# When the last LayerNorm sum is read, and where six h_lo subtractions stand in VectorE's queue

## The chip, the cores and the metric

One core of one Trainium2 chip. The metric is device time in microseconds, the median of several executions. TensorE (PE) multiplies, VectorE (DVE) and ScalarE (ACT) work elementwise, GpSimd (POOL) here does one kind of subtraction, and the sync engine (SP) issues most loads. The kernel is written engine by engine: each engine has a fixed list of instructions, and semaphores are the only thing that holds one engine for another.

## The reference

One mixer layer over x of 512 x 2048 floats, everything in fp32:

```python
h = rmsnorm(x, pre_norm_g)
q, fz, iv, gate_a, u, ug, gate_b = split(h @ w_in)            # 7 blocks of 1024 columns
# group A: 8 heads of a gated linear recurrence (HGRN2), d_k = d_v = 128
o_a = hgrn2(q, fz, iv, lower_bound) -> per-head rmsnorm * norm_g * silu(gate_a)
# group B: GLU, causal depthwise convolution of width 31, LayerNorm over the 1024 channels
a = u * sigmoid(ug);  y = conv31(a) + bias
o_b = silu((y - mean(y)) * rsqrt(var(y) + eps) * g + b) * silu(gate_b)
out = x + rmsnorm(concat(o_a, o_b) @ w_out, post_norm_g)
```

## The kernel before

**Precision.** Every large product runs as three fp32r products, hi x hi, hi x lo and lo x hi. Each operand is thus cut in two: ACT copies the raw tile to the `hi` tile (L374 for weights, L602 for the mixer's output) and a subtraction gives the `lo` tile (POOL L324 for weights, DVE L1011 in `mix_lo` for the mixer's output).

**Units.** Weights come as 144 units of 512 KB through a ring of four slots: 48 units for the convolution's channels (they also bring the value columns), 64 for the heads (8 a head), 32 for the output product (4 column blocks `c`, 8 units `s` each). A unit is 24 matmuls of 512 columns, issued 0.227 us apart. Per unit: SP loads it, ACT makes w_hi (`hi_unit`, two units ahead), POOL makes w_lo, PE multiplies.

**Stages.** (1) x is normalised and transposed; (2) convolution channels; (3) `head(0)` to `head(7)`: PE projects head h while the small matmuls of head h-1 (`slot(h-1, u)`) come after unit u, and DVE and ACT do that head's `late(h-1, u)` and their `own(h, u)`; (4) the output product, where the small matmuls of head 7 (`slot(7, s)`) come ahead of unit s of block c = 0.

**The LayerNorm statistics.** In head 0, at u = 5, DVE centres the 8 tiles (L781). At u = 6 and 7 ACT squares them one after the other (L459) into t1 and t2, and DVE adds them into t3 (L791, L789). The 8 adds count up `vacc_done`; t1 and t2 are used in turn, so each square waits for the add of the one before last. PE sums t3 over the partitions with an fp32 matmul against ones into bank 3 (L1253, `var_done`), and ACT turns that into 1/std in `lnr` (`ln_rstd`, L463 and L465). `lnr` is used first by DVE at u = 4 of head 1.

**Block c = 0 of the output product.** `mix` holds 16 tiles of the mixer's output. Tile `at` (in the order MIX_AT) becomes h_hi by ACT's `mix_hi(at)` (semaphore `mhi_done`) and h_lo by DVE's `mix_lo(at)` (`mlo_done`). Unit s of PE waits for `mlo_done >= 2 s + 2`. Meanwhile head 7 must be finished on the same engines. PE's `slot(7, s)` for s = 1, 2, 3 waits for `probs_done` counts 4, 6 and 12 of that head, which DVE reaches by copying masked scores out of PSUM (`take_scores`: L920 and L915 give 1 to 4, L928 gives 5 and 6, L935 gives 7 to 12, L941 the last). The last LayerNorm tile (`ln_tile(7, ...)`, DVE L799 to L814, ACT L472 to L480) runs between them. ACT's queue there is, in order: six L602; the gate (L539 to L382); L374, two L602 (tiles 6, 7); L374, L546, L548, two L602 (8, 9); L374, L551; L472, L473, L475, L477; two L602 (10, 11); L374; L480; one L602 (12).

Of the kernel before, what the change touches and what calls it, by code (L numbers as in the profile page):

```python
# [27 lines left out]
def build_layer(nc, x, pre_norm_g, post_norm_g, w_in, lb_logits, hg_norm_g, dw_kernel, dw_bias,  # L28
# [23 lines left out]
    CONV_U, HEAD_U = 2 * CONV_T, 2 * HEAD_T  # L52
# [36 lines left out]
    with ctx:  # L89
# [273 lines left out]
        def _(act):  # L363
# [97 lines left out]
            def ln_rstd():  # L461
                act.wait_ge(var_done, 1)
                A(lnr, bank(3), ACT.Ln, scale=1.0 / W_B, bias=EPSB).then_inc(lnr_s, 1)  # L463
                act.wait_ge(lnr_s, 1)
                A(lnr, lnr, ACT.Exp, scale=-0.5).then_inc(lnr_s, 1)  # L465

            def ln_tile(j, s):

                if s == 0:
                    act.wait_ge(gb_taken, j + 1)  # L470
                    act.wait_ge(ln_v, 7 * j + 2)
                    A(t3, t1, ACT.Abs).then_inc(ln_s, 1)  # L472
                    A(t4, gates[:, ds(j * T, T)], ACT.Abs).then_inc(ln_s, 1)  # L473
                    act.wait_ge(ln_s, 4 * j + 2)
                    A(part(2, 2), part(2, 2), ACT.Exp, scale=-1.0).then_inc(ln_s, 1)  # L475
                    act.wait_ge(ln_s, 4 * j + 3)
                    A(part(2, 2), part(2, 2), ACT.Ln, bias=1.0).then_inc(ln_s, 1)  # L477
                if s == 1:
                    act.wait_ge(ln_v, 7 * j + 5)
                    A(t3, t3, ACT.Exp).then_inc(ln_sig, 1)  # L480
# [53 lines left out]
            def late(g, u, first, last=False):  # L534
                if u == 0:
                    act.wait_ge(unit_done, N_HEAD + HEAD_U * (g + 1))
                    if not first:
                        act.wait_ge(head_done, g)
                    A(sgate, bank(1), ACT.Copy).then_inc(gate_taken, 1)  # L539
                    act.wait_ge(gate_taken, g + 1)  # L540
                    softplus_of_abs(sgate, t4, gate_s, 3 * g)
                if u == 1:
                    act.wait_ge(v_taken, H // 2)
                    if not first:
                        act.wait_ge(o_done, g)
                    A(vals, mix[:, ds(g * T, T)], ACT.Copy).then_inc(vals_ready, 1)  # L546
                    act.wait_ge(gate_ls, g + 1)
                    A(t4, t4, ACT.Exp).then_inc(gate_sig, 1)  # L548
                if u == 2:
                    act.wait_ge(kt_done, g + 1)  # L550
                    A(kdec[:, 0:T - P], XB[:, 0:T - P], ACT.Copy).then_inc(kt_taken, 1)  # L551
                if u == SQ_U:
                    act.wait_ge(o_done, g + 1)
                    act.wait_ge(gate_ready, g + 1)
                    act.wait_ge(ln_v, 7 * g + 6)
                    A(t4, OB, ACT.Square).then_inc(osq_done, 1)
                    if not last:
                        act.wait_ge(osq_done, 2 * g + 1)
                        A(sq_hi, t4, ACT.Copy).then_inc(osq_hi, 1)
                if u == 7:  # L560
                    act.wait_ge(norm_done, g + 1)
                    A(t1, XB, ACT.Ln, scale=1.0 / P, bias=EPSB).then_inc(rs_s, 1)
                    act.wait_ge(rs_s, 2 * g + 1)
                    A(t1, t1, ACT.Exp, scale=-0.5).then_inc(rs_s, 1)

            def head_step(h, u, q0, squares=None):
                base = N_HEAD + HEAD_U * h
                hi_unit(base + u + AHEAD, (u + AHEAD) % RING, q0 + (u + AHEAD) // RING,
                        squares=squares if u == SQ_U + 1 else None)
# [10 lines left out]
            def head_rest(h, first):  # L580
                for u in range(HEAD_U):
                    head_step(h, u, N_HEAD // RING + 2 * h, squares=h)
                    if first and u == 1:
                        ln_rstd()
                    late(h - 1, u, first)
                    own(h, u, False)
                    if u in (4, 5):
                        ln_tile(h - 1, u - 4)
# [66 lines left out]
        def _(dve):  # L655
# [137 lines left out]
            def ln_tile(j, s, first):  # L793
                y = mix[:, ds((H + j) * T, T)]
                gb = gates[:, ds(j * T, T)]
                if s == 0:
                    if first:
                        dve.wait_ge(lnr_s, 2)
                    V.tensor_copy(lnp[:, :], par3[:, TAPS + 1:TAPS + 3, j]).then_inc(ln_v, 1)  # L799
                    V.tensor_tensor(t1, y, lnr, ALU.mult).then_inc(ln_x, 1)  # L800
                    dve.wait_ge(ln_v, 7 * j + 1)
                    dve.wait_ge(ln_x, j + 1)
                    V.tensor_scalar(t1, t1, lnp[:, 0:1], lnp[:, 1:2], ALU.mult, ALU.add).then_inc(ln_v, 1)
                if s == 1:
                    dve.wait_ge(ln_s, 4 * (j + 1))
                    V.scalar_tensor_tensor(t3, t1, 0.0, t3, ALU.min, ALU.subtract).then_inc(ln_v, 1)
                    V.scalar_tensor_tensor(t4, gb, 0.0, t4, ALU.min, ALU.subtract).then_inc(ln_v, 1)
                    dve.wait_ge(ln_v, 7 * j + 4)
                    V.tensor_tensor(t3, t3, t4, ALU.add).then_inc(ln_v, 1)
                    V.tensor_tensor(t2, t1, gb, ALU.mult).then_inc(ln_v, 1)  # L810
                if s == 2:
                    dve.wait_ge(ln_sig, j + 1)
                    dve.wait_ge(ln_v, 7 * j + 6)
                    V.tensor_tensor(y, t2, t3, ALU.mult).then_inc(ln_v, 1)  # L814
# [192 lines left out]
            def mix_lo(at):  # L1007
                m = MIX_AT[at]
                dve.wait_ge(mhi_done, at + 1)
                a = slice(at * T, (at + 1) * T)  # L1010
                V.tensor_tensor(h_lo[:, a], mix[:, m * T:(m + 1) * T], h_hi[:, a].bitcast(fp32), ALU.subtract).then_inc(mlo_done, 1)  # L1011
# [9 lines left out]
                V.tensor_tensor(mix[:, tt * D + c * 512:tt * D + (c + 1) * 512], bank(4 * (c % 2) + tt),  # L1021
                                gates[:, c * 512:(c + 1) * 512], ALU.mult).then_inc(y_taken, 1)

            for at in range(4):
                mix_lo(at)
            for s in range(OUT_U):
                late(H - 1, s, False, last=True)
                if s == 1:
                    mix_lo(4)
                    mix_lo(5)  # L1030
                if s in (2, 3, 4):
                    ln_tile(J - 1, s - 2, False)
                for at in {2: (6, 7), 3: (8, 9), 4: (10, 11), 5: (12, 13), 6: (14,), 7: (15,)}.get(s, ()):
                    mix_lo(at)
            dve.wait_ge(gain_in, 32)
            for c in range(CHUNKS - 1):
# [16 lines left out]
        def _(pe):  # L1053
# [64 lines left out]
            def project(n, slot, half, b):  # L1118

                pe.wait_ge(lo_done, n + 1)  # L1120
                for k in range(HK):
                    kt = half * HK + k
                    wh = w_hi[:, slot * UW + k * P:slot * UW + (k + 1) * P]
                    wl = w_lo[:, slot * UW + k * P:slot * UW + (k + 1) * P]
                    hh, hl = h_hi[:, kt * T:(kt + 1) * T], h_lo[:, kt * T:(kt + 1) * T]
                    mm(bank(b), wh, hh, start=kt == 0, stop=False)  # L1126
                    mm(bank(b), wh, hl, start=False, stop=False)  # L1127
                    ins = mm(bank(b), wl, hh, start=False, stop=kt == KT - 1)  # L1128
                ins.then_inc(unit_done, 1)
# [105 lines left out]
            def head(h, first, second):  # L1235
                for u in range(HEAD_U):
                    if u == 0:
                        pe.wait_ge(ug_taken, J) if first else pe.wait_ge(gb_taken, h)
                    if u == 2:
                        pe.wait_ge(u_taken, J) if first else pe.wait_ge(gate_taken, h)  # L1240
                    if u == 4:
                        pe.wait_ge(f_v, 8 * h + 2)
                    if u == 6:
                        pe.wait_ge(q_taken, h + 1)
                    project(N_HEAD + HEAD_U * h + u, u % RING, u % 2, (u // 2) % 2)
                    if not first:
                        slot(h - 1, u, second)
                    if first and u == 4:
                        pe.wait_ge(ysum_done, J)
                        mm(bank(2), ones[:, :], lnr, start=True, stop=True).then_inc(mean_done, 1)  # L1250
                    if second and u == 0:
                        pe.wait_ge(vacc_done, J)
                        mm(bank(3), ones[:, :], t3, start=True, stop=True).then_inc(var_done, 1)  # L1253

# [65 lines left out]
```

## Time and profile before

| what | value |
|---|---|
| median of 3 runs | 890.32 us (890.29 to 892.9) |
| the profiled execution | 890.29 us, of it 888.3 us span from first to last instruction |
| PE busy | 872.4 us, 98% of the span |
| DVE busy | 567.7 us, 64% |
| ACT busy | 386.7 us, 44% |
| POOL busy | 363.5 us, 41%, of it 357.4 us in L324 |
| granted TensorE clock, mean | 0.992 |

The profile gives for each instruction its start, its length, and the idle time of its engine before it with what ended that. PEld is PE's weight load, which runs ahead of the matmul. Starts overlap the end of the instruction before by about 0.1 us on DVE and ACT. A matmul's length covers its way through the array; the step from one start to the next (0.227 us for 512 columns) is what it costs in a row.

### The profile page before, as it was taken

To read this page: it belongs to the slowest core of one execution; us is meant where nothing else is said; L and a number is where in the kernel's file an instruction comes from. 1 tells how busy PE (TensorE), PEld (TensorE's weight loads), DVE (VectorE), ACT (ScalarE), POOL (GpSimd) and SP (SyncE) were. 2 spreads that over 40 slices of the span, in tenths; PEclk is the share of its full clock that TensorE was granted. 3 is DMA by queue.
4 is the path that set the end of the run, shared out by engine and by line. 5 is a ranking of instruction groups with operands and counts; after the bars stand their busy time and mean duration, and the time that the engine had idled before them with its cause. 6 is when DMAs were issued, how large, how long until landed. Compare 5 with 4: busy or idle time off the path is not lost.

```text
span 888.3 us, 13244 instructions
## 1 busy us (share of the span) xinstructions
PE 872.4 (98%) x4616; PEld 747.8 (84%) x4616; DVE 567.7 (64%) x911; ACT 386.7 (44%) x585; POOL 363.5 (41%) x165
## 2 busy tenths in 40 slices
PE   6999999999999999999999999999999999999996
PEld 5998898898898888888888888888888888888885
DVE  6877786786786894775849486684948892010105
ACT  6433312312312455654746565573756743222221
POOL 3374444444444444352442435244242534444440
PEclk8999999999999999999999999999999999999999
DMA  9243233233233233132232314233132345433304
GB/s 317 69 128 102 80 104 103 78 104 102 77 105 101 78 95 96 48 116 74 72 94 70 96 47 121 68 88 91 57 94 63 101 140 209 153 100 101 101 5 190
DMA packets 119703, 89.70 MB, mean 101 GB/s; under 512 B 2640, under 2 KB 109433, under 8 KB 118137
## 3 DMA queue, kind: packets, MB, share of 16 engines
q1 hardware_dynamic: 118921, 84.04, 31.1%
q10 hardware_dynamic: 752, 5.25, 1.6%
q8 instruction: 20, 0.33, 0.1%
q14 instruction: 10, 0.08, 0.0%
HBM read 85.09 MB, written 4.19 MB: 101 GB/s over the span
## 4 chain that ended last, share of the span: by engine, by line
PE 96%; DVE 3%; DMA 1%; ACT 0%; DVEq 0%; issue 0%; ACTq 0%
PE banks L1128 19%; PE banks L1126 19%; PE banks L1127 19%; PE banks L1268 7%; PE banks L1267 7%; PE banks L1266 7%; PE banks L1143 3%; PE banks L1142 3%; PE banks L1141 3%; DVE mix L666 1%; PE banks L1187 1%; PE banks L1177 1%; PE banks L1193 1%; PE banks L1221 1%; DVE mix L671 1%; PE banks L1196 1%
## 5 line engine op out<-in xcount | busy, mean ns | idle before, releaser
L324 POOL TENSOR_TENSOR w_lo<-w_raw,w_hi 128x1024 fp32r<-128x1024 f32 x144 | 357.4, 2485 | 497.9 <-ACT w_hi L374 497.8
L1126 PE MATMUL banks<-h_hi,w_hi 128*128 128x512 f32 x736 | 291.2, 396 | 0.0
L1128 PE MATMUL banks<-h_hi,w_lo 128*128 128x512 f32 x736 | 286.7, 390 | 0.0
L1127 PE MATMUL banks<-h_lo,w_hi 128*128 128x512 f32 x736 | 286.6, 389 | 0.0
L374 ACT ACTIVATE w_hi<-w_raw 128x1024 fp32r<-128x1024 f32 x144 | 151.6, 1053 | 260.6 <-PE banks L1268 100.0
L734 DVE SCALAR_TENSOR_TENSOR banks<-work,tap,banks 128x512 f32<-128x512 f32 x232 | 175.3, 756 | 8.0
L1128 PEld LDWEIGHTS banks<-h_hi,w_lo 128*128 128x128 f32 x736 | 138.2, 188 | 29.1
L1127 PEld LDWEIGHTS banks<-h_lo,w_hi 128*128 128x128 f32 x736 | 138.3, 188 | 27.9 <-issue 0.5
L1126 PEld LDWEIGHTS banks<-h_hi,w_hi 128*128 128x128 f32 x736 | 138.3, 188 | 27.8 <-issue 0.5
L1266 PE MATMUL banks<-w_hi,h_hi 128*128 128x512 f32 x256 | 100.6, 393 | 0.0
L1268 PE MATMUL banks<-w_hi,h_lo 128*128 128x512 f32 x256 | 99.7, 389 | 0.0
L1267 PE MATMUL banks<-w_lo,h_hi 128*128 128x512 f32 x256 | 99.6, 389 | 0.0
L1142 PE MATMUL banks<-w_lo,h_hi 128*128 128x256 f32 x256 | 72.4, 283 | 0.0
L1143 PE MATMUL banks<-w_hi,h_lo 128*128 128x256 f32 x256 | 72.4, 283 | 0.0
L1141 PE MATMUL banks<-w_hi,h_hi 128*128 128x256 f32 x256 | 72.4, 283 | 0.0
L1021 DVE TENSOR_TENSOR mix<-banks,gates 128x512 f32<-128x512 f32 x16 | 11.0, 689 | 85.6 <-PE banks L1268 85.6
L1267 PEld LDWEIGHTS banks<-w_lo,h_hi 128*128 128x128 f32 x256 | 48.1, 188 | 10.1 <-issue 0.2
L1266 PEld LDWEIGHTS banks<-w_hi,h_hi 128*128 128x128 f32 x256 | 48.1, 188 | 10.1 <-issue 0.2
L1268 PEld LDWEIGHTS banks<-w_hi,h_lo 128*128 128x128 f32 x256 | 48.1, 188 | 9.9
L1141 PEld LDWEIGHTS banks<-w_hi,h_hi 128*128 128x128 f32 x256 | 49.1, 192 | 0.3
L1142 PEld LDWEIGHTS banks<-w_lo,h_hi 128*128 128x128 f32 x256 | 49.1, 192 | 0.3
L1143 PEld LDWEIGHTS banks<-w_hi,h_lo 128*128 128x128 f32 x256 | 49.1, 192 | 0.0
(176 smaller groups left out, 927.8 us busy)
## 6 DMA issues: line engine op xcount, KB each, us to landing
w_raw<-in_w_in SPq DMA_DIRECT2D x112, 512.0 KB, 3.7
w_raw<-in_w_out SPq DMA_DIRECT2D x32, 512.0 KB, 3.8
mix<-in_x SPq DMA_DIRECT2D x4, 1024.0 KB, 7.8
work<-in_x ACTq DMA_DIRECT2D x4, 1024.0 KB, 9.8
out_y<-mix SPq DMA_DIRECT2D x3, 1024.0 KB, 3.9
gates<-in_post_norm_g ACTq DMA_DIRECT2D x1, 1024.0 KB, 5.4
out_y<-mix SPq DMA_DIRECT2D x4, 256.0 KB, 2.7
work<-in_dw_kernel SPq DMA_DIRECT2D x1, 64.0 KB
```

The costliest lines, as they stand in the source:

```text
L324: g.tensor_tensor(w_lo[:, a], w_raw[:, a], w_hi[:, a].bitcast(fp32), ALU.subtract).then_inc(lo_done, 1)
L374: A(w_hi[:, a], w_raw[:, a], ACT.Copy).then_inc(hi_done, 1)
L734: V.scalar_tensor_tensor(dst, src, tp[:, w:w + 1], acc, ALU.mult, ALU.add).then_inc(tap_done, 1)
L1126: mm(bank(b), wh, hh, start=kt == 0, stop=False)
L1127: mm(bank(b), wh, hl, start=False, stop=False)
L1128: ins = mm(bank(b), wl, hh, start=False, stop=kt == KT - 1)
L1141: mm(o, h_hi[:, a], w_hi[:, w], start=vu == 0 and k == 0, stop=False)
L1142: mm(o, h_hi[:, a], w_lo[:, w], start=False, stop=False)
L1143: ins = mm(o, h_lo[:, a], w_hi[:, w], start=False, stop=vu == 3 and k == VK - 1)
L1266: mm(o, h_hi[:, a], w_hi[:, w], start=s == 0 and k == 0, stop=False)
L1267: mm(o, h_hi[:, a], w_lo[:, w], start=False, stop=False)
L1268: ins = mm(o, h_lo[:, a], w_hi[:, w], start=False, stop=s == OUT_U - 1 and k == 1)
```

## The change

Three edits. (a) PE reads t3 for the variance at the end of head 0 (after unit 7) instead of behind the first small matmuls of head 1; ACT's `ln_rstd` moves with it, from u = 1 to u = 0 of head 1, where it stands ahead of the gate work of `late(0, 0)`. (b) DVE makes the h_lo tiles 4 and 5 ahead of `late(7, 1)`, not behind it. (c) Behind the score copies of s = 1 DVE now makes four tiles (6 to 9), at s = 2 tiles 10 and 11, at s = 3 tile 12, at s = 5 tiles 13 and 14.

```diff
@@ ACT, head_rest
-                    if first and u == 1:
+                    if first and u == 0:
                         ln_rstd()
                     late(h - 1, u, first)
@@ DVE, output stage
-            for at in range(4):
+            for at in range(6):
                 mix_lo(at)
             for s in range(OUT_U):
                 late(H - 1, s, False, last=True)
-                if s == 1:
-                    mix_lo(4)
-                    mix_lo(5)
                 if s in (2, 3, 4):
                     ln_tile(J - 1, s - 2, False)
-                for at in {2: (6, 7), 3: (8, 9), 4: (10, 11), 5: (12, 13), 6: (14,), 7: (15,)}.get(s, ()):
+                for at in {1: (6, 7, 8, 9), 2: (10, 11), 3: (12,), 5: (13, 14), 7: (15,)}.get(s, ()):
                     mix_lo(at)
@@ PE, head
-                    if second and u == 0:
+                    if first and u == HEAD_U - 1:
                         pe.wait_ge(vacc_done, J)
                         mm(bank(3), ones[:, :], t3, start=True, stop=True).then_inc(var_done, 1)
```

PE at the border from head 0 to head 1, before: the variance matmul (L1253) stands behind the 24 matmuls of head 1's first unit (L1126 to L1128) and the first small matmuls (L1177).

```order
L1128 MATMUL banks<-h_hi,w_lo 128x512
L1177 MATMUL banks<-near,work 128x192 [waits lev_ready]
L1177 MATMUL banks<-near,work 128x192 x3
L1253 MATMUL banks<-work,ones 128x512 [waits vacc_done]
L1126 MATMUL banks<-h_hi,w_hi 128x512 [waits lo_done]
```

The same engine now (lines are three lower): the variance matmul (L1250) is the first thing behind the last unit of head 0.

```order
L1124 MATMUL banks<-h_lo,w_hi 128x512
L1125 MATMUL banks<-h_hi,w_lo 128x512
L1250 MATMUL banks<-work,ones 128x512 [waits vacc_done]
L1123 MATMUL banks<-h_hi,w_hi 128x512 [waits lo_done,gb_taken]
L1124 MATMUL banks<-h_lo,w_hi 128x512
```

One matmul with its wait has moved ahead of 24 large and 4 small ones.

DVE from the start of the output stage, before: L1011 makes the h_lo tiles, L920, L915, L928 and L935 copy scores.

```order
L1011 TENSOR_TENSOR h_lo<-mix,h_hi 128x512 [waits mhi_done] x4
L948 SCALAR_TENSOR_TENSOR work<-work 128x512 [waits gate_s]
...
L1011 TENSOR_TENSOR h_lo<-mix,h_hi 128x512 [waits mhi_done] x2
L951 TENSOR_TENSOR work<-work 128x512 [waits gate_sig]
L928 COPY work<-banks 64x4x64 [waits masks_ready,probs_done,lev_done]
...
L803 TENSOR_SCALAR work<-work,lnp 128x512 [waits ln_x,ln_v]
L1011 TENSOR_TENSOR h_lo<-mix,h_hi 128x512 [waits mhi_done] x2
L935 COPY_PREDICATED work<-mask,banks 128x8x24 [waits masks_ready,probs_done,lev_done]
```

The same engine now:

```order
L1011 TENSOR_TENSOR h_lo<-mix,h_hi 128x512 [waits mhi_done] x6
L948 SCALAR_TENSOR_TENSOR work<-work 128x512 [waits gate_s]
...
L1011 TENSOR_TENSOR h_lo<-mix,h_hi 128x512 [waits mhi_done] x4
L951 TENSOR_TENSOR work<-work 128x512 [waits gate_sig]
L928 COPY work<-banks 64x4x64 [waits masks_ready,probs_done,lev_done]
...
L803 TENSOR_SCALAR work<-work,lnp 128x512 [waits ln_x,ln_v]
L1011 TENSOR_TENSOR h_lo<-mix,h_hi 128x512 [waits mhi_done] x2
L935 COPY_PREDICATED work<-mask,banks 128x8x24 [waits masks_ready,probs_done,lev_done]
```

Two more subtractions stand ahead of L948 and two more, four in all, ahead of L951 and L928. The two ahead of L935 look the same but are other tiles: 10 and 11 now, 6 and 7 before.

## Rows read from the trace of the kernel before

**Rows 1.** PE's waits: engine, line <- what it waited for: us, times, longest.

```profile
PE banks L1071 <- DVE mix L666: 4.9, 3, 2.0
PE banks L1059 <- POOL ident L316: 1.7, 1, 1.7
PE banks L1093 <- DVE mix L671: 1.4, 1, 1.4
PE banks L1071 <- DVE mix L671: 0.4, 1, 0.4
```

**Rows 2.** Timeline, head 0 to 1: start, us, engine, line [idle before <- releaser].

```profile
334.15 2.57 POOL L324 TENSOR_TENSOR w_lo<-w_raw,w_hi 128x1024 fp32r<-128x1024 f32 x1 [5.19 <-ACT w_hi L374]
334.63 2.64 DVE L789 TENSOR_TENSOR work<-work 128x512 f32<-128x512 f32 x1 [0.17 <-ACT work L459]
...
337.92 0.19 PEld L1126 LDWEIGHTS banks<-h_hi,w_hi 128*128 128x128 f32 x1
338.14 0.39 PE L1126 MATMUL banks<-h_hi,w_hi 128*128 128x512 f32 x1
...
338.97 0.69 DVE L789 TENSOR_TENSOR work<-work 128x512 f32<-128x512 f32 x1
...
344.72 0.35 PEld L1253 LDWEIGHTS banks<-work,ones 128*128 128x128 f32 x2
```

**Rows 3.** Timeline of ACT and DVE at the start of head 1.

```profile
339.65 0.57 ACT L539 ACTIVATE work<-banks 128x512 f32<-128x512 f32 x1
...
342.32 0.69 DVE L948 SCALAR_TENSOR_TENSOR work<-work 128x512 f32<-128x512 f32 x1 [2.66 <-ACT work L382]
...
345.15 0.73 DVE L920 COPY_PREDICATED work<-mask,banks 128x256 f32<-128x256 int8 x1 [2.13 <-PE banks L1177]
...
345.94 0.69 ACT L463 ACTIVATE work<-banks,epsb 128x512 f32<-128x512 f32 x1 [2.76 <-PE banks L1253]
346.66 0.63 ACT L465 ACTIVATE work<-work 128x512 f32<-128x512 f32 x1
```

**Rows 4.** Source view of L1187: lengths in ns, first and last start.

```profile
L1187 PEld LDWEIGHTS banks<-work x64: 187/190/190, 357.9 to 712.9; 128*128 128x128 f32 x64
```

**Rows 5.** Timeline of DVE in the first part of the output stage.

```profile
697.52 2.48 DVE L1011 TENSOR_TENSOR h_lo<-mix,h_hi 128x512 fp32r<-128x512 f32 x4
701.04 0.69 DVE L948 SCALAR_TENSOR_TENSOR work<-work 128x512 f32<-128x512 f32 x1 [1.04 <-ACT work L382]
...
704.15 3.64 DVE L1011 TENSOR_TENSOR h_lo<-mix,h_hi 128x512 fp32r<-128x512 f32 x2
707.72 2.87 DVE L951 TENSOR_TENSOR work<-work 128x512 f32<-128x512 f32 x1
710.52 1.23 DVE L928 COPY work<-banks 64x256 f32<-64x256 f32 x3
...
714.42 2.35 DVE L935 COPY_PREDICATED work<-mask,banks 128x192 f32<-128x192 int8 x6
```

**Rows 6.** Timeline of POOL in the same stretch.

```profile
702.04 8.00 POOL L324 TENSOR_TENSOR w_lo<-w_raw,w_hi 128x1024 fp32r<-128x1024 f32 x3 [5.46 <-ACT w_hi L374]
```

**Rows 7.** Timeline of PE at its second and third group of small matmuls.

```profile
711.80 0.46 PEld L1187 LDWEIGHTS banks<-work 128*128 128x128 f32 x3 [0.15 <-DVE work L928]
...
718.66 0.55 PE L1196 MATMUL banks<-work 128*128 128x64 f32 x4
```

**Rows 8.** Timeline of ACT from the LayerNorm tile to h_hi tiles 10 and 11.

```profile
713.28 0.63 ACT L472 ACTIVATE work<-work 128x512 f32<-128x512 f32 x1 [5.93 <-DVE work L803]
...
716.53 1.14 ACT L602 ACTIVATE h_hi<-mix 128x512 fp32r<-128x512 f32 x2
```

**Rows 9.** Windows: stretch, us, busy us (instructions) of PE, PEld, DVE, ACT, POOL; PEclk; DMA.

```profile
14.00:18.00 4.00, 1.97 (x8) 1.57 (x8) 4.00 (x4) 1.63 (x2) 3.36 (x2) 0.57 1.06 360
18.00:22.00 4.00, 3.41 (x16) 3.42 (x17) 4.00 (x5) 3.86 (x7) 0.00 (x0) 0.50 1.10 285
22.00:26.00 4.00, 4.00 (x25) 4.00 (x25) 4.00 (x3) 3.94 (x7) 2.88 (x1) 0.65 0.40 140
```

## The prediction

> **What bounds the kernel now.** I read the engines' shares first: PE is busy nearly all of the span, DVE two thirds, ACT and POOL less than half. Then PE's waits [rows 1]: there are four entries, and all of them belong to lines of the first stage (warm-up, transposes, the first projection). From the convolution to the end of the output product no matmul is listed as waiting for anything. So PE's list of matmuls is the length of the kernel, nothing can be gained by making another engine earlier, and every microsecond in which PE is made to wait is added to the end one for one. The change touches three places of that stretch. I therefore ask at each one when DVE, ACT and POOL deliver now, and by how much PE's need lies behind that. All times below are on the time axis of the profile before; a delay of PE moves everything behind it alike, since loads, ACT, POOL and DVE all follow PE's counts.
>
> **Part 1, the variance matmul.** Head 0's last matmul is followed by head 1's first, whose weights are loaded at 337.92 and which starts at 338.14 [rows 2]. There PE will now wait for the eighth add. The last L789 starts at 338.97 and takes 0.69, so it ends at 339.66 [rows 2]. It is that late because the chain of squares and adds is serial and one add of it took 2.64 instead of 0.69: it came while POOL's subtraction ran (334.15 to 336.72) and ended 0.55 after it [rows 2]. All this lies ahead of the first moved instruction, so it stays. A release shows as a weight load about 0.06 later, and the fp32 matmul starts 0.1 to 0.2 behind that load. So the matmul starts at about 339.88 where head 1 would have started at 338.14: a wait of 1.74 us, call it **+1.7**. The matmul itself costs the same in either place. Behind the waiting instruction are queued the 24 matmuls of head 1's first unit and all after them.
>
> Bounds of this term: 0, if the add were not held by POOL (its 2.0 us gone, the chain would end at about 337.7), and 1.9. I take 1.7, because the rows of this very chain show it.
>
> ACT's part: `ln_rstd` now waits ahead of L539. From the load of the variance matmul to L463 it was 1.22 (344.72 to 345.94), and L463 and L465 end 1.35 after that [rows 2, 3]. With the load at 339.72, L463 starts at 340.94 and ACT comes to L539 at 342.3 instead of 339.65 [rows 3], 2.65 later. Who waits for that: DVE's L948 goes from 342.32 to 344.97 and ends at 345.66, still ahead of L920, which waits for PE and starts at 345.15 + 1.7 [rows 3]. The next w_hi, and so POOL's w_lo, also come 2.65 later; they belong to unit 3 of head 1, which PE starts only behind the small matmuls L1187, the first of which are at 357.9 [rows 4], over ten microseconds of cover. The copy of the gate bank is needed by unit 2, further off too. Cost **0**; if that cover were gone it would be at most 2.65. Having `lnr` earlier gains nothing, since it is used at u = 4.
>
> **Part 2, tiles 4 and 5 ahead of the gate.** Four L1011 started at 697.52 and took 2.48, 0.60 apart, and then DVE was idle for 1.04 until the gate's L382 was done [rows 5]. Two more end at 701.20, so L948 starts at 701.12 instead of 701.04: 0.08 late. The four score copies behind it end 0.08 later, at 704.4. PE needs them for the small matmuls one unit ahead of L1187: 711.8 [rows 7] less 24 x 0.227 = 5.4 and less some 1.3 for those matmuls, about 705.0. Cost **0**: what hides it is DVE's idle time. The two that stood behind the copies are gone from there.
>
> **Part 3, four tiles where two were.** Behind the copies two L1011 took 3.64 and then L951 took 2.87 [rows 5]. Undisturbed they take 0.6 to 0.7 each. POOL ran three subtractions in a row there; together they end at 710.04, and L951 ends 0.55 behind them at 710.59 [rows 5, 6]. So one DVE subtraction gets through behind each POOL subtraction. This is the pattern of Part 1 again.
>
> The Trainium skill has a rule for it ("SBUF — State Buffer", Who interferes with whom): a DVE instruction with two SBUF inputs contends with a GpSimd instruction that reads SBUF, and the loser is blocked until the other is through. The trace agrees: 2.87 in place of 0.68. By the rule alone, were each of the two added subtractions to meet a POOL instruction of its own, Part 3's first step would be 5.6 us. The row shows only three POOL instructions, so the sum does not take that.
>
> With four L1011: the first ends near 705.0 and the second at 707.79, as the two do now; the third takes L951's place behind POOL's last and ends at 710.59; the fourth adds 0.60, and L951 in its new place 0.60 again, now with POOL idle. L928's three copies end at 711.75 + 1.20 = 712.95. PE has no margin at all here: its weight load for L1187 was released by L928 (0.15 idle on PEld) [rows 7]. So the wait is **+1.2** one for one. It is 1.5 if POOL's second subtraction now wins the race for the first L1011, which comes 0.08 later. It is 0 if POOL did not disturb DVE.
>
> Then `ln_tile(7, 0)` is 1.20 later too: L472 at 714.48 in place of 713.28 [rows 8]. Next in DVE's queue is the added wait: tiles 10 and 11. Before, tiles 6 and 7 stood there, long ready. ACT makes h_hi 10 and 11 only behind L472 to L477; its second L602 ended at 716.53 + 1.14 = 717.67 [rows 8], now 718.87. DVE sits idle from about 714.4, makes the two tiles, and is done at 719.6. Behind this wait on DVE are queued the six L935 (2.35 for all [rows 5]), which PE needs for L1196. They start at about 719.5 and end at 721.9. PE's L1196 started at 718.66 [rows 7] and will start at 721.88 + 0.06 + 0.11 = 722.05. That is 3.39 late, of which 1.20 is the wait before: **+2.2**. If the first step were 0, the same chain gives 717.4 for the copies and no wait, so this term's bounds are 0 and 2.5.
>
> After that nothing is near. PE's next wait on DVE is at s = 5, two units or 10.9 us behind L1196; DVE has nine short instructions for it, some 5 us, and even with two of them held by POOL (2.2 each more) it is done within 10. Tiles 10 and 11 are there for unit 5 anyway. The end of the kernel is untouched.
>
> **Sum.** The profiled execution took 890.29 (span 888.3 and 2.0 around it), which is the median of before within 0.03. 890.29 + 1.74 + 0 + 0 + 3.39 = **895.4**.
>
> **Rivals.**
> - *The first wait is not there*, because the one add slips ahead of POOL's subtraction. POOL had started 0.48 before it [rows 2], and nothing ahead of it changes. Then 890.3 + 3.4 = 893.7. Chance 0.07.
> - *The output stage hides its part*: this decides on whether POOL's three subtractions meet the four L1011. If not, tile 9 is bound by ACT at about 706, L928 ends by 708.4, L935 by 717.4 and PE waits for neither. Then only Part 1 is left: 892.0, not slower by what can be told. Against it: the two L1011 and L951 of before were each held there. Chance 0.08.
> - *Nothing is seen at all*, 890.3: DVE has a third of its time free, and somewhere the delays are absorbed. This would need PE to have had waits that shrink, and [rows 1] has none behind the first stage. Chance 0.04. The Trainium skill ("Perfetto Trace Analysis", Identifying the Most-Contended Engine) says to look at the engine with the highest occupancy; by that rule a reordering on DVE would not move the time. The rows on PE's zero margin speak against it.
> - *The clock falls during the waits.* In the first stage, with 1.97 us busy in 4, PE's granted clock fell from 1.00 to 0.50 (1.2 of 2.4 GHz) and came back within 22 to 26 [rows 9]. What was lost: 0.43 x 4 + 0.50 x 4 + 0.35 x 4 = 5.1 us. That gives 900.5. Against it: there PE had been idle again and again, half of the time from 14 to 18; here waits of 1.2 and 2.2 have a fully busy unit between them. Chance 0.07.
> - *Faster*: I find no mechanism, since PE has no wait to lose. Chance 0.02.
>
> **How the numbers follow.** The forecast has 0.72. Its own range is 895.0 to 896.5 (the race, the small lags). The range given goes down to take in the first rival, with the smaller values of its terms, and up for the race lost and the scatter of the runs: 893.0 to 897.5. It leaves out the output stage hidden (0.08), nothing seen (0.04), the clock (0.07) and faster (0.02). A measurement of this kernel can tell about 0.3% (2.7 us) from no change, so slower begins at 893.0: 0.72 + 0.07 + 0.07 = 0.86. Within 0.3%: 0.08 + 0.04 = 0.12. Faster: 0.02.
>
> **What would show it.** PE's waits should have three new entries: the variance matmul on L789, about 1.7; L1184 (the former L1187) on L928, about 1.2; L1193 (the former L1196) on L935, about 2.2. DVE should show an idle time of about 4 before an L1011, ended by ACT's L602, and one more L1011 of 2.87. L951 should be 0.69 long. POOL idle behind L803 and a granted clock of 1.00 throughout. If L951 is still 2.87 long, a fourth POOL subtraction lies there and I have counted it wrong; if the wait before an L1011 is missing, I have misread ACT's order.

## The result, and the profile after

| kernel | median us | runs | span |
|---|---|---|---|
| before | 892.76 | 5 (890.29 to 893.04) | |
| changed | 899.6 | 5 (896.96 to 901.2) | |
| before, profiled | 890.29 | | 888.3 |
| changed, profiled | 898.06 | | 896.0 |

The ratio is 1.0074, with a 95% interval of 1.0056 to 1.0091: the change costs 6.6 us (5.0 to 8.1), where 5.1 was forecast. It is slower, as forecast, but 899.6 lies outside the range given, 893.0 to 897.5. The medians hide the reason, the single times show it: before comes in two groups, near 890.4 and near 892.9, and the median that I started from was of three runs, two of which were in the lower group. One later execution of before, of 1255.61 us at a granted clock of 0.653, is counted nowhere below.

PE's waits in the changed kernel answer to [rows 1]; lines of the output stage and of PE are three lower than before.

```profile
PE banks L1068 <- DVE mix L666: 6.1, 3, 3.3
PE banks L1193 <- DVE work L935: 2.0, 1, 2.0
PE banks L1056 <- POOL ident L316: 1.7, 1, 1.7
PE banks L1090 <- DVE mix L671: 1.4, 1, 1.4
PE banks L1250 <- DVE work L789: 1.4, 1, 1.4
PE banks L1068 <- DVE mix L671: 1.4, 1, 1.4
PE banks L1184 <- DVE work L928: 0.8, 1, 0.8
```

There are three new waits, at the three places forecast: L1250 (the variance matmul), L1184 and L1193. This view gives them 1.4, 0.8 and 2.0, each 0.3 less than the delay that the start times below show. But the two entries of L1068, in the first stage, have also grown, from 4.9 to 6.1 and from 0.4 to 1.4, and the change does not touch that stage.

The best way to see where time goes on an engine that is never idle is to compare the start of the same instruction in both traces. These are the weight loads of matmuls that stand at fixed places, from the source views: first of the kernel before, then of the changed one. "A to B" is the start of the first and of the last instance.

```profile
L1250 PEld LDWEIGHTS banks<-work,ones x2: 187/188/188, 320.7 to 320.9; 128*128 128x128 f32 x2
L1177 PEld LDWEIGHTS banks<-near,work x64: 187/190/190, 343.4 to 699.2; 128*128 128x128 f32 x64
L1196 PEld LDWEIGHTS banks<-work x64: 187/192/192, 364.7 to 719.3; 128*128 128x128 f32 x64
L1228 PEld LDWEIGHTS banks<-work,ones x2: 187/188/188, 738.0 to 738.2; 128*128 128x128 f32 x2
```

```profile
L1247 PEld LDWEIGHTS banks<-work,ones x2: 187/188/188, 323.3 to 323.5; 128*128 128x128 f32 x2
L1174 PEld LDWEIGHTS banks<-near,work x64: 187/190/190, 348.6 to 703.5; 128*128 128x128 f32 x64
L1184 PEld LDWEIGHTS banks<-work x64: 186/190/190, 362.2 to 718.3; 128*128 128x128 f32 x64
L1193 PEld LDWEIGHTS banks<-work x64: 186/192/192, 369.0 to 727.0; 128*128 128x128 f32 x64
L1225 PEld LDWEIGHTS banks<-work,ones x2: 187/188/188, 745.7 to 745.9; 128*128 128x128 f32 x2
```

The mean's matmul, ahead of everything that was changed, is at 323.3 instead of 320.7: +2.6 from the first stage. The last small matmuls ahead of the output stage are at 703.5 instead of 699.2: +4.3, so 1.7 for the variance matmul. The last L1184 is at 718.3, where its L1187 was at 712.9 [rows 4]: +5.4, so 1.1 more. The last L1193 is at 727.0 instead of 719.3: +7.7, so 2.3 more. Behind that nothing: +7.7 at L1225, and +7.7 in the span. The change's own part is 1.7 + 1.1 + 2.3 = 5.1.

DVE in the output stage, the rows that answer to [rows 5]:

```profile
701.85 3.69 DVE L1011 TENSOR_TENSOR h_lo<-mix,h_hi 128x512 fp32r<-128x512 f32 x6
705.46 0.68 DVE L948 SCALAR_TENSOR_TENSOR work<-work 128x512 f32<-128x512 f32 x1
...
708.57 6.96 DVE L1011 TENSOR_TENSOR h_lo<-mix,h_hi 128x512 fp32r<-128x512 f32 x4
715.45 0.68 DVE L951 TENSOR_TENSOR work<-work 128x512 f32<-128x512 f32 x1
716.05 1.09 DVE L928 COPY work<-banks 64x256 f32<-64x256 f32 x3
...
722.58 1.29 DVE L1011 TENSOR_TENSOR h_lo<-mix,h_hi 128x512 fp32r<-128x512 f32 x2 [3.98 <-ACT h_hi L602]
723.90 2.30 DVE L935 COPY_PREDICATED work<-mask,banks 128x192 f32<-128x192 int8 x6
```

The signs that the prediction named are here, but for one: it wanted a granted clock of 1.00 throughout, and in this execution the clock is at 1.00 at the three new waits but not in the first stage. Six subtractions fill the gap ahead of L948. Four take 6.96, the length of two free ones (0.6 to 0.7) and two held ones (2.87); L951 has lost its hold (0.68, was 2.87). DVE then stands idle for 3.98 until ScalarE's L602, with the six score copies queued behind.

### The profile page after: what moved, and what is told of

The parts are those of the page before. It is cut to its first block, busy times and chain, and to the rows that moved or that the text cites. A ratio compares the mean times of both kernels' runs of the same rounds, so it can differ in the third digit from the quotient of the medians.

```text
span 896.0 us, 13244 instructions
## 1 busy us (share of the span) xinstructions
PE 873.6 (97%) x4616; PEld 747.8 (83%) x4616; DVE 566.1 (63%) x911; ACT 386.8 (43%) x585; POOL 361.9 (40%) x165
## 4 chain that ended last, share of the span: by engine, by line
PE 88%; DVE 8%; ACT 1%; issue 1%; DMA 1%; DVEq 0%; ACTq 0%
PE banks L1123 17%; PE banks L1125 17%; PE banks L1124 17%; PE banks L1265 6%; PE banks L1263 6%; PE banks L1264 6%; PE banks L1140 3%; PE banks L1139 3%; PE banks L1138 3%; DVE mix L666 1%; DVE h_lo L1011 1%; PE banks L1184 1%; PE banks L1174 1%; PE banks L1218 1%; PE banks L1193 1%
```

## The experiments

### What the first stage does: fillers in TensorE's idle times

In the first 20 us TensorE waits again and again for DVE, and its clock falls. I put 44 transposes of the identity into those waits (16, 8, 10 between the halves of a block, 10); what they write is overwritten later. `before_fill` (e1) has them in the kernel before, `after_fill` (e2) in the changed one.

```diff
+            def fill(n, to):
+                for _ in range(n):
+                    nc.tensor.transpose(to[:, 0:P], ident[:, :], ident[:, :])
...
+            fill(16, OB)
             x_transposes(0, 0)
             pe.wait_ge(gain_col, 1)
-            x_transposes(1, 0)
+            fill(8, bank(3))
+            x_transposes(1, 0, 10)
+            pe.wait_ge(x_norm, 2)
+            fill(10, OB)
             pe.wait_ge(x_norm, 4)
```

> The kernel before, with 44 filler transposes on TensorE put into its idle times of the first 20 us (16 behind the gain transpose, 8 ahead of the second block's transposes, 10 between its halves, 10 ahead of the first projection); their output is overwritten. Theory S (the scatter of 890.3 to 893.0 of before, and the part of after above 895.4, come from when TensorE's clock falls in the first stage): with no idle stretch of over 1 us the granted clock stays at 1.00 from 2 to 30 us, the times lie within 1 us of each other, and the kernel gains some 2.5 to 5 us on the 890.3 of before (half the 10 us of low clock at 14.6 to 24.6, less what DVE bounds there). Rival T (the scatter comes from loads or from later stages): the clock still falls or the times still scatter by 2 to 3 us.

> The changed kernel with the same 44 filler transposes. Theory S: its time is that of the filled kernel before plus 5.1 us (1.7 at the variance matmul, 1.2 and 2.2 in the output stage) with little scatter. Rival U (the change costs 6.8 us, the difference of the medians, because something beside the three waits was added): 6.5 or more between the two filled kernels.

Windows of the changed kernel's first stage, then of the filled kernel before. The columns are: stretch, us, busy us (instructions) of PE, PEclk, DMA share, GB/s for the second, and with all five engines for the first.

```profile
8.00:12.00 4.00, 2.61 (x12) 2.61 (x13) 2.02 (x3) 3.81 (x7) 0.00 (x0) 0.51 1.18 336
12.00:16.00 4.00, 1.96 (x11) 1.59 (x10) 4.00 (x3) 2.00 (x2) 3.62 (x2) 0.50 1.01 420
16.00:20.00 4.00, 3.02 (x13) 2.21 (x12) 4.00 (x4) 1.06 (x1) 1.17 (x1) 0.50 1.15 291
```

```profile
8.00:12.00 4.00, 2.93 (x28) 1.00 1.18 336
12.00:16.00 4.00, 3.18 (x28) 1.00 1.01 420
16.00:20.00 4.00, 3.01 (x25) 1.00 1.16 295
```

In the changed kernel's trace the clock is at 0.5 (1.2 GHz) from 8 on; in the trace of before it was at 1.00 until 14. With fillers it stays at 1.00. Where the two traces part, first before, then changed:

```profile
1.70 5.38 PE L1059 MATMUL banks<-ident 128*128 128x128 f32 x24 [1.70 <-POOL ident L316]
9.34 1.97 PE L1071 MATMUL banks<-ident,mix 128*128 128x128 f32 x16 [2.05 <-DVE mix L666]
11.62 3.51 DVE L666 TENSOR_SCALAR mix<-mix,rst 128x1024 f32<-128x1024 f32 x2
18.59 0.58 PE L1093 MATMUL banks<-h_hi,w_hi 128*128 128x256 f32 x1 [1.43 <-DVE mix L671]
```

```profile
1.70 4.25 PE L1056 MATMUL banks<-ident 128*128 128x128 f32 x24 [1.70 <-POOL ident L316]
9.39 3.68 PE L1068 MATMUL banks<-ident,mix 128*128 128x128 f32 x16 [3.28 <-DVE mix L666]
12.54 5.18 DVE L666 TENSOR_SCALAR mix<-mix,rst 128x1024 f32<-128x1024 f32 x2
21.18 0.58 PE L1090 MATMUL banks<-h_hi,w_hi 128*128 128x256 f32 x1 [1.43 <-DVE mix L671]
```

The 24 warm-up transposes took 4.25 us instead of 5.38 (why, the traces do not show), so TensorE was idle for 3.28 ahead of x's transposes instead of 2.05, and the clock fell in that idle time. Then x's 16 transposes took 3.68 instead of 1.97, and VectorE came to its second pair of scalings 0.9 later. There GpSimd's subtractions held both instead of one (5.18 against 3.51), which adds 1.7. Together that is the 2.6 by which the first projection starts later, 21.18 against 18.59. No execution of before in its upper group was profiled; this reading rests on the changed kernel, whose first stage has the same instructions.

| kernel | times |
|---|---|
| before, 27 executions beside e5 to e8 | 9 from 890.15 to 890.54 (clock 0.990 to 0.992), 18 from 892.82 to 893.25 (0.987 to 0.990) |
| before_fill, 8 | 7 from 890.18 to 890.65, one 892.08; median 890.38, ratio to before 0.9979 (0.9968 to 0.999) |
| after_fill, 6 | 895.41, 895.42, 895.49 and 896.92, 896.94, 897.06 |

The scatter was forecast right but for one execution of eight (892.08, not explained; the longest wait left with fillers is 1.8 us, not under 1). The gain was not: I had expected 2.5 to 5 us below 890.3, and the filled kernel is at 890.38. The ratio of 0.9979 is against a median of before beside it of 892.91, with 9 of 13 executions in the upper group. Beside the last two experiments, on another chip, it was 5 of 14. So the low clock from 14 on costs nothing, because there DVE sets the pace: the first projection starts at 18.66 with fillers and started at 18.59 without. Only the earlier fall, at 8, costs: TensorE's transposes are then late enough to hold up DVE, and DVE meets GpSimd once more. Start-up without the early fall is 890.4, with it 892.9.

That leaves a second scatter in after_fill, 895.4 or 897.0, where e2 had expected little. Its median, 896.21, is 5.8 above the filled kernel before, between the 5.1 of my theory and the 6.5 of the rival, so that e2 alone decides nothing. Windows of its profiled execution, which took 897.06, around the wait for L935:

```profile
722.00:724.00 2.00, 0.28 (x3) 1.00 0.00 0
724.00:726.00 2.00, 2.00 (x15) 0.69 0.32 82
726.00:728.00 2.00, 2.00 (x6) 0.50 0.58 186
728.00:730.00 2.00, 2.00 (x10) 0.96 0.01 2
```

The clock falls behind that wait and is back some 3 to 4 us later. In the profiled execution of the changed kernel, with a wait of the same length, it does not:

```profile
724.00:728.00 4.00, 1.97 (x17) 1.00 0.06 6
```

### The waits of the output stage, one at a time

Both kernels make tiles 4 and 5 early, as in edit (b), and leave the variance matmul as before. `lo_four` has four subtractions behind the first copies, but tiles 10 and 11 behind the L935 copies. `lo_late` has two behind the first copies, as many as before, and 8 to 11 ahead of the L935 copies. The line of each is marked with its name.

```diff
-                for at in {2: (6, 7), 3: (8, 9), 4: (10, 11), 5: (12, 13), 6: (14,), 7: (15,)}.get(s, ()):
+                for at in {1: (6, 7, 8, 9), 3: (10, 11), 4: (12,), 5: (13, 14), 7: (15,)}.get(s, ()):   # lo_four
+                for at in {1: (6, 7), 2: (8, 9, 10, 11), 3: (12,), 5: (13, 14), 7: (15,)}.get(s, ()):   # lo_late
```

> The kernel before with tiles 4 and 5 early, four tiles (6 to 9) behind the copies of s = 1, but tiles 10 and 11 at s = 3 behind ln_tile, not at s = 2; the variance matmul as before. My theory: TensorE waits 0.8 to 1.2 us for L928 (two more held subtractions ahead of it) and not at all for L935; no wait at the variance matmul. Rival (the second wait is only the first one grown): a wait for L935 of 1 us or more although tiles 10 and 11 are gone from ahead of it.

> The kernel before with tiles 4 and 5 early, two tiles (6, 7) behind the copies of s = 1 as many as before, and four (8 to 11) at s = 2. My theory: no wait for L928 beyond 0.2 us, and one for L935 of 2.0 to 2.3 us, because tile 11 must wait for ScalarE's copy behind L477; VectorE idle some 3 us ahead of an L1011. Rival (queue length alone does it): the wait for L935 is under 1 us, since two more subtractions with GpSimd idle take only 1.2 us and the copies had 1.9 us to spare.

The waits of PE behind the first stage: in lo_four one,

```profile
PE banks L1184 <- DVE work L928: 0.8, 1, 0.8
```

and in lo_late the other.

```profile
PE banks L1193 <- DVE work L935: 1.9, 1, 1.9
```

DVE in lo_late shows the cause of the second. Two subtractions run at once, then it waits for ScalarE:

```profile
713.05 1.29 DVE L1011 TENSOR_TENSOR h_lo<-mix,h_hi 128x512 fp32r<-128x512 f32 x2
717.12 1.29 DVE L1011 TENSOR_TENSOR h_lo<-mix,h_hi 128x512 fp32r<-128x512 f32 x2 [2.79 <-ACT h_hi L602]
718.45 2.31 DVE L935 COPY_PREDICATED work<-mask,banks 128x192 f32<-128x192 int8 x6
```

The two waits are independent, as forecast: one comes from subtractions ahead of L928 that GpSimd holds, the other from subtractions ahead of L935 whose input is not made. So the second wait does not need the first: in lo_late L951 is held as before (2.88), L928 is in time, and L935 is late all the same. There is one execution of each, so the parts are read from the traces. lo_four took 894.13, which is 892.9 + 1.2 with the early fall of the clock (its transposes of the first block took 3.68, as in the changed kernel's trace). lo_late took 894.12: 890.3 + 2.2, and 1.6 more, because in its trace the clock fell behind the wait (0.75 and 0.50 from 720 to 724). The same total has different parts; a single time could not have told them apart.

### Keeping TensorE busy in the new waits

The changed kernel with start-up fillers, and with 10, 8 and 16 more ahead of the three waits. The waits are not shortened, they are only not idle.

```diff
+                if last and u in (2, 3):
+                    pe.wait_ge(head_done, g)
+                    fill((8, 16)[u - 2], OB)
                 if 1 <= u <= 3:
                     pe.wait_ge(probs_done, COPIES * g + (4, 6, 12)[u - 1])
...
                     if first and u == HEAD_U - 1:
+                        pe.wait_ge(v_taken, J // 2)
+                        fill(10, OB)
                         pe.wait_ge(vacc_done, J)
```

> The changed kernel with the start-up fillers and with filler transposes ahead of its three new waits too: 10 ahead of the variance matmul, 8 ahead of the small matmuls that wait for L928, 16 ahead of those that wait for L935. The waits stay as long as they are (VectorE sets them), TensorE is only not idle in them. Theory C (the upper of the two groups of times, 895.4 and 897.0, is a fall of TensorE's clock behind the wait for L935, worth 1.6 us): all executions lie within 0.7 us of 895.4, the granted clock is 1.00 from 700 to 860. Rival D (the 1.6 us come from something else that varies, as a load or a subtraction of GpSimd): half of them stay at 897.

Seven executions lie from 895.34 to 895.58, median 895.45. The upper group is gone, so it was the clock. (Of after_fill 3 of 6 executions lay in the upper group, of lo_only below 7 of 10; here it is none of 7.) And with both of the clock's effects out, the change costs 895.45 - 890.38 = 5.1 us. Its windows:

```profile
722.00:724.00 2.00, 1.72 (x16) 1.00 0.00 0
724.00:726.00 2.00, 2.00 (x17) 1.00 0.29 78
```

### The two parts alone, and why the variance matmul waits

All three kernels have the start-up fillers. `var_only` has edit (a), `lo_only` has (b) and (c). `var_unheld` has (a), and the w_hi that ScalarE makes at u = 7 of head 0 comes behind its squares instead of ahead of them.

```diff
             for u in range(HEAD_U):
-                head_step(0, u, N_HEAD // RING)
+                if u < 7:
+                    head_step(0, u, N_HEAD // RING)
...
                         ln_square(j)
+                if u == 7:
+                    head_step(0, u, N_HEAD // RING)
```

> The kernel before with start-up fillers and the variance matmul moved (with ScalarE's ln_rstd), the output stage as before. My theory: one new wait, 1.4 us on the matmul and 1.7 us of time in all, 892.1 against 890.4 of the filled kernel before; no second group of times, since the clock does not fall behind so short a wait. Rival (PE's delay is absorbed later, or ScalarE's later gate work adds a wait of its own): 890.4, or 893 and more.

> As the run before, but ScalarE makes the w_hi of head 0's u = 7 behind its four squares instead of ahead of them, so that GpSimd's subtraction no longer runs while VectorE adds the squares. Theory P (the variance matmul waits because one add was held by GpSimd for 2.0 us): no add of 2.6 us in the chain, the wait at the variance matmul is 0 to 0.2 us and the time is 890.4 to 890.7. Rival Q (the chain of squares and adds is too long anyway): a wait of over 1 us remains and the time is 891.5 or more.

> The kernel before with start-up fillers and the new places of the h_lo subtractions alone, the variance matmul as before. My theory: waits of 0.8 for L928 and 2.0 for L935, 3.4 us of time, so 893.8, and 895.4 in those executions in which the clock falls behind the second wait. Rival (the parts interact, the first wait of the whole change shifts GpSimd against VectorE): a sum other than 3.4.

| kernel | times | less 890.38 |
|---|---|---|
| var_only, 10 executions | 9 from 891.95 to 892.15, one 893.74; median 892.08 | 1.7 |
| var_unheld, 10 | 890.32 to 890.54, median 890.44 | 0.1 |
| lo_only, 10 | 3 from 893.66 to 893.78, 7 from 895.17 to 895.55 | 3.3 and 4.9 |

PE's waits behind the first stage: var_only has this one, var_unheld has none.

```profile
PE banks L1263 <- DVE work L789: 1.4, 1, 1.4
```

The last four adds of the chain on DVE, in var_only and in var_unheld (there L792), and GpSimd's next subtraction in var_unheld, which now comes behind them:

```profile
334.63 5.03 DVE L789 TENSOR_TENSOR work<-work 128x512 f32<-128x512 f32 x4 [0.17 <-ACT work L459]
```

```profile
334.56 3.07 DVE L792 TENSOR_TENSOR work<-work 128x512 f32<-128x512 f32 x4
```

```profile
337.80 4.76 POOL L324 TENSOR_TENSOR w_lo<-w_raw,w_hi 128x1024 fp32r<-128x1024 f32 x2 [8.63 <-ACT w_hi L374]
```

5.03 against 3.07: the 2.0 us of one held add were the whole wait. (The 893.74 of var_only was not forecast; see below.) The parts add up: 1.7 + 3.3 = 5.0, against 5.1 for both.

### A version that beats both

In the filled kernel DVE sets the first stage, and its scalings of x are held by GpSimd in the same way. Here GpSimd's first two subtractions wait until the second block of x is scaled, the third until the third block is, the fourth until the last is, with fillers (`before_best`) and without (`before_pool`).

```diff
             for n in range(PEEL * RING):
+                if n in (0, 2, 3):
+                    pool.wait_ge(x_scaled, (4, 0, 6, 8)[n])
                 lo_unit(n, n % RING)
```

> The kernel before with start-up fillers, and with GpSimd's first subtractions held back: units 0 and 1 start when the second block of x is scaled, unit 2 when the third is, unit 3 when the fourth is. Theory H (in the filled kernel the first stage is set by VectorE, whose scalings of x are held by GpSimd three times for about 2.1 us each): the first scaling of 2.9 us is gone, the first projection starts 2 us earlier, at about 16.6, and the kernel takes 887.5 to 888.5. Rival (the later low parts now hold the projections instead): 890.4 or more, with waits of the projections for GpSimd.

> The same hold-back of GpSimd without fillers, the kernel before otherwise. Theory S with H: two groups of times again, each about 2 us below 890.4 and 892.9, since the clock still falls in the first stage. Rival (the low clock no longer matters once GpSimd is out of the way, since VectorE then has slack for it): one group.

The second pair of scalings on DVE, in the filled kernel before and in before_best:

```profile
11.69 3.52 DVE L666 TENSOR_SCALAR mix<-mix,rst 128x1024 f32<-128x1024 f32 x2
```

```profile
11.67 1.41 DVE L668 TENSOR_SCALAR mix<-mix,rst 128x1024 f32<-128x1024 f32 x2
```

And the first projection of before_best:

```profile
16.85 0.39 PE L1101 MATMUL banks<-h_hi,w_hi 128*128 128x256 f32 x1 [0.23 <-DVE mix L673]
```

before_best takes 887.71 (887.61 to 887.83, 5 runs), ratio to before 0.9962 (0.9947 to 0.9977): the fastest kernel of the study, 2.9 us below the 890.62 of before beside it, and 2.7 us below their lower group (890.28 to 891.0). The expectation held (the first projection starts 1.8 us earlier, where 2 was expected). A new wait of 0.8 for GpSimd's w_lo has come, as the rival said, but it is smaller than the gain. before_pool takes 888.41 (887.57 to 888.99, 9 runs), ratio 0.9966 (0.9955 to 0.9977). There I was wrong: the two groups 2.5 us apart are gone, and one spread of 1.4 is left, though in the one trace the clock still falls (0.58 from 10 to 12, 0.57 from 12 to 14, then back at 1.00). With GpSimd out of its way DVE has no scaling that a late start can push into a hold. That fits the traces of the first stage above, where 1.7 of the 2.6 us were a hold more; that each execution of before_pool has its fall is not shown.

## Why the prediction was wrong in its time and right in what the change costs

**What bounds the kernel: right where the change is, wrong for the first stage.** Every delay of PE reached the end one for one. But "nothing can be gained by making another engine earlier" is false: PE waits for 8.4 us in the first stage [rows 1], and before_best, in which VectorE's scalings come earlier, is 2.7 us faster than the lower group of before. The same overlooked stage is what moved the time.

**Part 1: right.** +1.7 forecast, 1.7 measured in the traces and 1.7 by var_only. Its cause is shown, not argued: unheld, the term is 0.1. ScalarE's later gate work cost nothing, as said; no wait for it appears.

**Part 2: right.** Nothing, by L948 directly behind six subtractions.

**Part 3: right in both waits.** +1.2 and +2.2 forecast, 1.1 and 2.3 in the traces, 3.3 together by lo_only. lo_four and lo_late show each with its own cause. The lower bound of the second term was argued with a first step of 0; lo_late has no first wait and the second at its full length, so that bound would need GpSimd's holds gone too.

**The sum: right as a difference (5.1), wrong as a time.** The step that failed is its first term: "The profiled execution took 890.29 (span 888.3 and 2.0 around it), which is the median of before within 0.03." That was two runs out of three. Of the 27 executions beside e5 to e8, 18 are near 892.9, and of all 54 later ones 32. The groups differ in the first stage, by 2.6 us in the traces. The row that should have warned me is the third time of the table, 892.9, and [rows 9]: I read the fall of the clock there as the price of a rival and did not ask whether the fall itself comes at the same time in each execution. From 892.8 the sum would have given 897.9; the other 1.6 us up to the measured 899.6 are the next point. In all, 890.3 + 5.1 + 2.6 + 1.6 = 899.6.

**The rival of the clock, left out of the sum: wrong in both chance and price.** I gave "The clock falls during the waits" 0.07 and 5.1 us. It fell in 3 of 6 executions of after_fill and in 7 of 10 of lo_only, by the gap between their groups, and cost 1.6 us. The price was mis-sized because I took the low stretch of the first stage, where TensorE goes on being idle; and as before_fill shows, that stretch, priced at 5.1, costs the kernel before nothing that can be measured. Behind a single wait the clock is back within some 3 to 4 us. The chance was mis-sized because I argued from the busy unit between the waits.

Together this accounts for the medians. The changed kernel has 5.1 us more, and on top of it a fall of the clock in over half of its executions: 895.5 (3 executions), 897.1 (4), 898.0 (6) and 899.6 (10) hold 23 of its 27, one group for each combination of the two falls (890.4 or 892.9, + 5.1, + 0 or 1.6). For before the four would be two. Of these groups only the one at 898.0 was profiled, so the others are assigned by their sums. The four that are left, 898.5 to 898.8 and 901.2, would be 1.6 above 897.1 and 899.6, as after one fall more; no trace shows it. What is not shown is why the clock falls in one execution and not in the next, with waits of the same length.

## What to carry to other kernels

When one engine is never idle, take for each moved instruction the moment at which that engine needs its result, and the state of every input that the moved instruction itself needs: here two subtractions queued ahead of work that TensorE waited for cost 2.3 us, because their own input was not there. A subtraction on DVE with two SBUF inputs costs 0.68 us alone and 2.87 behind GpSimd, so its price depends on where in GpSimd's schedule it lands. And before a sum is added to a baseline, look whether the single times of the baseline form groups; with three runs, one that is 0.3% off may be the commoner case.

## What the hardware showed that I had not expected

- Behind one wait of 2.0 us, between long stretches in which TensorE was fully busy, the granted clock fell to 0.50 and was back within some 3 to 4 us, at a cost of 1.6 us, in some executions and not in others. Behind the wait of 1.4 us one of ten executions of var_only was 1.7 us above the rest; it was not the execution profiled, so that this too was the clock is not shown.
- In the first stage the clock fell at about 8 us in some executions and at 14 in others. The earlier one came where the same 24 warm-up transposes had taken 4.25 us and not 5.38, with an idle time of 3.28 us behind them and not 2.05. It cost 2.5 us (2.6 in the traces: 0.9 in slower transposes, 1.7 in a VectorE scaling pushed under a GpSimd subtraction); the later fall cost nothing that can be measured.
- VectorE's scalings of x (one SBUF tensor, 128x1024) are held by GpSimd's subtraction just as the additions are: a pair took 3.52 us beside it and 1.41 with GpSimd held back.
- Fillers on TensorE cost nothing where they fit into a wait: with 44 of them the median is 890.38, that of the lower group of before, and the times of the changed kernel with 78 lie within 0.24 us of each other.
